# Latent attention of the odd layer: keys and values as products of the weight stream, heads as steps beside gates and output product

## What is computed

```python
cq, ckv, ik, iw, gate = _split_cols(z, [Q_LORA, KV_LORA, IDX_DIM, IDX_HEADS, DSA_WIDTH])
q = (_rmsnorm(cq, q_norm) @ w_qb).reshape(b, t, 16, 128)
q_lat = jnp.einsum('bthd,hdc->bthc', q, w_uk)
ckv = _rmsnorm(ckv, kv_norm)
# for each query the 64 tokens with the highest index score, among those not later than it
s = jnp.einsum('bqhc,bqkc->bqhk', q_lat, ckv[sel]) * 128 ** -0.5
p = softmax(s)
o_lat = jnp.einsum('bqhk,bqkc->bqhc', p, ckv[sel])
o = jnp.einsum('bthc,hcd->bthd', o_lat, w_uv).reshape(b, t, 2048)
return (o * jax.nn.silu(gate)) @ w_out
```

## Time and profile before

| | us |
|---|---|
| median of 3 runs | 2896.55 (2895.43 to 2902.48) |
| the profiled execution | 2893.83 |
| its span, first to last instruction | 2892.0 |
| mean granted clock of TensorE | 0.998 of 2.4 GHz |
| busy: PE, DVE, ACT, POOL | 2857.4, 1879.2, 1417.9, 393.4 |
| transfers | 192 GB/s over the span |

### The profile page before, as it was taken

The page is one execution under the profiler, slowest core; times in us unless marked ns, Lnnn a source line. Parts: engine busy times, 40 slices in busy tenths (PEclk is TensorE's granted clock), DMA queues, the critical chain, the costliest instruction groups (busy, mean ns, idle before and its releaser), DMA issues.

```text
span 2892.0 us, 45428 instructions
## 1 busy us (share of the span) xinstructions
PE 2857.4 (99%) x19064; PEld 2606.1 (90%) x19064; DVE 1879.2 (65%) x2575; ACT 1417.9 (49%) x1964; POOL 393.4 (14%) x444
## 2 busy tenths in 40 slices
PE   8999999999999999999999999999999999999998
PEld 8999988998899988989998899898889999988997
DVE  6998655766566655778666666588555555555555
ACT  5445645456455555444444445654545444444444
POOL 0000000000000000008873663043000000000000
PEclk9999999999999999999999999999999999999999
DMA  7555455552555545567776666585655555555553
GB/s 244 190 195 172 155 189 187 188 178 74 187 195 172 171 168 175 193 202 248 238 245 216 231 230 211 186 258 165 204 190 184 195 191 194 198 190 192 197 194 131
DMA packets 288043, 558.45 MB, mean 193 GB/s; under 512 B 27424, under 2 KB 35872, under 8 KB 287584
## 3 DMA queue, kind: packets, MB, share of 16 engines
q1 hardware_dynamic: 281376, 531.27, 55.7%
q0 software_dynamic: 5456, 21.73, 1.9%
q10 hardware_dynamic: 1008, 2.55, 0.3%
HBM read 530.34 MB, written 25.17 MB: 192 GB/s over the span
## 4 chain that ended last, share of the span: by engine, by line
PE 92%; DVE 4%; ACT 2%; issue 1%; POOL 0%; DMA 0%; ACTq 0%; DVEq 0%; POOLq 0%
PE G L506 86%; PE T L506 4%; DVE WL L1648 1%; ACT WH L1071 1%; DVE Y L1656 1%; PE T L585 1%; PE G L979 0%; ACT SC_e L1074 0%; DVE X L1648 0%; DVE ST L1729 0%; DVE SC_e L1656 0%; ACT L1068 0%; POOL ZZ L2428 0%; DMA X<-in_x 0%; PE T L964 0%
## 5 line engine op out<-in xcount | busy, mean ns | idle before, releaser
L1648 DVE TENSOR_TENSOR WL<-RAW,WH 128x1024 fp32r<-128x1024 f32 (+1 forms) x948 | 1183.8, 1258 | 754.7 <-ACT WH L1071 745.3
L1071 ACT ACTIVATE WH<-RAW 128x1024 fp32r<-128x1024 f32 (+1 forms) x948 | 993.8, 1055 | 1027.4 <-PE G L506 1025.5
L506 PE MATMUL G<-A1h,WH 128*128 128x256 f32 (+1 forms) x2583 | 717.9, 279 | 1.6 <-DVE WL L1648 1.6
L506 PE MATMUL G<-A1l,WH 128*128 128x256 f32 x2560 | 710.7, 278 | 0.0
L506 PE MATMUL G<-A1h,WL 128*128 128x256 f32 x2560 | 709.4, 277 | 0.0
L506 PEld LDWEIGHTS G<-A1h,WH 128*128 128x128 f32 x2583 | 485.7, 188 | 5.1 <-DVE WL L1648 2.9
L506 PEld LDWEIGHTS G<-A1l,WH 128*128 128x128 f32 x2560 | 482.3, 188 | 0.4
L506 PEld LDWEIGHTS G<-A1h,WL 128*128 128x128 f32 x2560 | 482.4, 188 | 0.0
L506 PE MATMUL G<-WH,Bh 128*128 128x512 f32 x1024 | 399.3, 390 | 0.6 <-DVE WL L1648 0.6
L506 PE MATMUL G<-WH,Bl 128*128 128x512 f32 x1024 | 398.5, 389 | 0.0
L506 PE MATMUL G<-WL,Bh 128*128 128x512 f32 x1024 | 398.5, 389 | 0.0
(11 more groups left out here) (325 smaller groups left out, 3564.6 us busy)
## 6 DMA issues: line engine op xcount, KB each, us to landing
RAW<-in_mlp_w SPq DMA_DIRECT2D x256, 1024.0 KB, 5.4
RAW<-in_even_w_in SPq DMA_DIRECT2D x52, 1024.0 KB, 5.0
RAW<-in_a_w_in SPq DMA_DIRECT2D x48, 1024.0 KB, 5.2
RAW<-in_b_w_glu SPq DMA_DIRECT2D x32, 1024.0 KB, 5.4
RAW<-in_odd_w_in SPq DMA_DIRECT2D x20, 1024.0 KB, 5.0
RAW<-in_even_w_out SPq DMA_DIRECT2D x16, 1024.0 KB, 5.1
RAW<-in_odd_w_out SPq DMA_DIRECT2D x16, 1024.0 KB, 5.1
RAW<-in_a_w_out SPq DMA_DIRECT2D x16, 1024.0 KB, 5.0
```

The costliest lines, as they stand in the source:

```text
L506: return e.matmul(out, lhsT, rhs, start=start, stop=stop, skip_group_check=True)
L1071: return e.activation(out, in_, ACT.Copy, scale=scale, bias=0.0)
L1648: return e.tensor_tensor(out, a, b, op)
```

## The change

Keys and values of four heads at a time become products `kk0` to `kk3` and `vv0` to `vv3` of the weight stream, one half each, with the latent in two parts (`CKTh`, `CKTl`). A chunk holds the key weights of four heads in its first half and their value weights in the second. For a key half PE transposes the weights from `RAW` to two of the banks `T` (`turn_keys`, steps in `gate1` and after it), and ACT and DVE split from there; a value half is split as any other. ACT evacuates both to `KTo` and `VO`, which now hold all heads. The order is `gate1`, `kk0`, `vv0`, ... `vv3`, `gate2`, `gate3`, `oo0`. The heads are steps beside the halves from `kk2` on, one slot of `HEADS_O` behind each: the scores of the heads in slots 0, 1, 3, 4, 6, 7, ... 15, 16, 18, 19, 20, 21, the shares one slot later, turn two and output three slots later. Slots 20 to 27 fall in `oo0`. The bank pairs are dealt in the other order up to `gate3`.

```diff
-    turn = itertools.cycle((0, 2))
+    turn = itertools.cycle((2, 0))
...
+    def latent_weights(g):
+        for tag, fm in ((f"kk{g}", True), (f"vv{g}", False)):
+            first_chunk[tag], STEPS[tag] = len(chunks), 1
+            bank = next(turn)
+            G_of[tag] = G[bank:bank + 2]
+            SHAPE[tag] = (2, 512, fm, [0])
+        second_half.add(f"vv{g}")
+        latent_chunk[len(chunks)] = g
+        chunks.append((None, (4, 512), True))
...
-    for i in range(1, 4):
+    weights("gate1", wo, 2048, 848 + 512, fm=True, steps=1)
+    for g in range(4):
+        latent_weights(g)
+    for i in range(2, 4):
         weights(f"gate{i}", wo, 2048, 848 + 512 * i, fm=True, steps=1)
-    next(turn)
...
-    HEADS_O = [{k: r - d for k, d in (("weights", 0), ("keys", 1), ("scores", 2), ("turn", 3), ("values", 3), ("pv", 4))
-                if 0 <= r - d < 16} for r in range(20)]
+
+    HEADS_O = [[] for _ in range(28)]
+    for _h, _n in enumerate((0, 1, 3, 4, 6, 7, 9, 10, 12, 13, 15, 16, 18, 19, 20, 21)):
+        for _d, _s in ((2, "turn"), (3, "pv"), (0, "scores"), (1, "shares")):
+            HEADS_O[_n + _d].append((_s, _h))
...
-        for i in range(1, 4):
-            if i == 3:
-                beside(first_rounds_o())
+        def heads_o():
+            for steps in HEADS_O:
+                for what, h in steps:
...
+                    fresh[0] = True
+                yield
+
+        def turn_keys():
+            for g in (None, 0, None, 1, None, None, None, 2, None, 3):
+                if g is not None:
+                    T, c = TB[2 * (g % 2):2 * (g % 2) + 2], first_chunk[f"kk{g}"]
+                    if g < 2:
+                        e.wait_ge(*o_d["ix", 13 + 2 * g])
+                    else:
+                        e.wait_ge(*w_lo[first_half(f"kk{g - 2}")])
+                    e.wait_ge(*w_in[c % NR][c])
+                    for j in range(2):
+                        for h in range(4):
+                            at = 256 * h + 128 * j
+                            m = e.transpose(T[j][:, 128 * h:128 * h + 128], RAW[:, c % NR, at:at + 128], IDENT)
+                    m.then_inc(*uk_t.up(g))
+                    fresh[0] = True
+                yield
+
...
+        beside(turn_keys())
+        gemm("gate1", A1h, A1l)
+        for g in range(4):
+            if g == 2:
+                finish()
+                beside(heads_o())
+            gemm(f"kk{g}", CKTh, CKTl, None if g else (lambda kt: e.wait_ge(*o_l["ckt"])))
+            gemm(f"vv{g}", CKTh, CKTl)
+        for i in range(2, 4):
             gemm(f"gate{i}", A1h, A1l)
-        finish()
-        for heads in HEADS_O[3:16]:
-            round_o(heads)
-        beside(last_rounds_o())
         for i in range(4):
-            if i == 1:
-                e.wait_ge(*k_c[15])
             gemm(f"oo{i}", A2ho, A2lo, None if i else (lambda kt: e.wait_ge(*o_l["o", kt])))
             beside(norm_block("a", i, f"oo{i}"))
         finish()
...
+            if n in key_half:
+                T = TB[2 * (key_half[n] % 2):2 * (key_half[n] % 2) + 2]
+                e.wait_ge(*uk_t[key_half[n]])
+                e.wait_ge(*w_read[n - RS])
+                copy(WH[:, n % RS, 0:512], T[0][:, :])
+                copy(WH[:, n % RS, 512:1024], T[1][:, :]).then_inc(*w_hi.up(n))
+                return
+            if h == 0 or c < NR or c in latent_chunk:
...
+        def latent(g):
+            gemm(f"kk{g}")
+            take_fm(f"kk{g}", KTo, 4 * g)
+            gemm(f"vv{g}")
+            for i in range(2):
+                e.wait_ge(*whole_bank(f"vv{g}", i))
+                copy(VO[:, 4 * g:4 * g + 4, i, :], G_of[f"vv{g}"][i][:, :].rearrange("p (h d) -> p h d", d=128)).then_inc(
+                    *ev_a.up((f"vv{g}", i)))
+
+        gemm("gate1")
+        silu_fm("gate1", GT, 4)
+        for g in range(4):
+            if g == 2:
+                beside(heads_o())
+            latent(g)
+        for i in range(2, 4):
             gemm(f"gate{i}")
...
-        finish()
-        for heads in HEADS_O[3:16]:
-            round_o(heads)
-        beside(last_rounds_o())
...
+            if n in key_half:
+                T = TB[2 * (key_half[n] % 2):2 * (key_half[n] % 2) + 2]
+                for j in range(2):
+                    d = tt(WL[:, n % RS, 512 * j:512 * j + 512], T[j][:, :], hi[:, 512 * j:512 * j + 512], ALU.subtract)
+                d.then_inc(*w_lo.up(n))
+                return
...
+        def heads_o():
+            for steps in HEADS_O:
+                for what, h in steps:
+                    st = 8 + 8 * (h % 2)
+                    if what == "scores":
+                        if h >= 2:
+                            e.wait_ge(*p_t["o", h - 2])
+                        maxima(TB[0], PP[h % 2], MM[:, :], st, ("o", h))
+                    elif what == "shares":
+                        shares(PP[h % 2], st, ("o", h))
+                    elif what == "pv":
+                        e.wait_ge(*pv_mm["o", h])
+                        if h % 4 == 0:
+                            e.wait_ge(*act2[f"gate{h // 4}", 1])
+                        tt(GT[:, h, :], TB[3][:, 0:256], GT[:, h, :], ALU.mult).then_inc(*o_d.up(("o", h)))
+                        e.wait_ge(*o_h["o", h])
+                        low(A2lo[:, h, :], GT[:, h, :], A2ho[:, h, :]).then_inc(*o_l.up(("o", h)))
...
-        for i in range(1, 4):
-            if i == 3:
+        gemm("gate1")
+        take_fm("gate1", GT, 4)
+        for g in range(4):
+            if g == 2:
                 finish()
-                beside(first_rounds_o())
+                beside(heads_o())
+            gemm(f"kk{g}")
+            gemm(f"vv{g}")
...
             take_fm(f"gate{i}", GT, 4 * i)
-        finish()
-        for heads in HEADS_O[3:16]:
-            round_o(heads)
         tt(GP, col("final", 0, 16), col("norm_mix", 0, 16), ALU.mult).then_inc(*d_step.up("gp"))
-        beside(last_rounds_o())
...
+            if c in latent_chunk:
+                g = latent_chunk[c]
+                e.dma_start(RAW[:, c % NR, 0:1024].rearrange("p (h c) -> p h c", c=256),
+                            t["odd_w_uk"][0, 4 * g:4 * g + 4].rearrange("h d c -> d h c")).then_inc(*w_in[c % NR].up(c, 16))
+                for k in range(2):
+                    at = 1024 + 512 * k
+                    e.dma_start(RAW[:, c % NR, at:at + 512].rearrange("p (h d) -> p h d", d=128),
+                                t["odd_w_uv"][0, 4 * g:4 * g + 4, 128 * k:128 * k + 128].rearrange("h p d -> p h d")).then_inc(
+                        *w_in[c % NR].up(c, 16))
+                return
```

More of the change, by code:

```diff
@@ L771, in pe @@
         finish()
[L773 to L828, removed]
@@ L1312, in prep_o @@
                     e.wait_ge(*t_mm["ckv"])
-                    copy(CKT[:, :, :], pairs(TB[2][:, :])).then_inc(*a_step.up("ckt"))
+                    copy(CKTh[:, :, :], pairs(TB[2][:, :])).then_inc(*o_h.up("ckt"))
                 elif what == "turn_ik":
@@ L1328, in act @@
             take_fm(f"qb{i}", QTo, 4 * i)
[L1330 to L1343, removed]
-                copy(KTo[h % 2], G[0][:, 0:256]).then_inc(*k_c.up(h))
-            if "turn" in heads:
-                h = heads["turn"]
-                e.wait_ge(*p_t["o", h])
-                if h >= 2:
-                    e.wait_ge(*pv_mm["o", h - 2])
-                copy(PT[h % 2], TB[1][:, 0:384]).then_inc(*p_c.up(("o", h)))
-            if "scores" in heads:
-                h = heads["scores"]
-                exps(PP[h % 2], 8 + 8 * (h % 2), ("o", h))
-            if "pv" in heads:
-                h = heads["pv"]
-                e.wait_ge(*o_d["o", h])
-                copy(A2ho[:, h, :], GT[:, h, :]).then_inc(*o_h.up(("o", h)))
-            if "values" in heads:
-                h = heads["values"]
-                e.wait_ge(*v_mm[h])
-                if h >= 2:
-                    e.wait_ge(*pv_mm["o", h - 2])
-                copy(VO[h % 2], TB[2][:, 0:256].rearrange("p (a b) -> p a b", b=128)).then_inc(*v_c.up(h))
@@ L1365, in first_rounds_o @@
-        def first_rounds_o():
-            for r in range(3):
-                yield
-                round_o(HEADS_O[r])
-                yield
-        def last_rounds_o():
-            for heads in HEADS_O[16:]:
-                round_o(heads)
-                yield
-        for i in range(1, 4):
-            if i == 3:
-                beside(first_rounds_o())
+        def heads_o():
+            for steps in HEADS_O:
+                for what, h in steps:
+                    if what == "turn":
+                        e.wait_ge(*p_t["o", h])
+                        if h >= 2:
+                            e.wait_ge(*pv_mm["o", h - 2])
+                        copy(PT[h % 2], TB[1][:, 0:384]).then_inc(*p_c.up(("o", h)))
+                    elif what == "scores":
+                        exps(PP[h % 2], 8 + 8 * (h % 2), ("o", h))
+                    elif what == "pv":
```

(6 more changed lines are left out.)

95 lines of the change are left out of this document (38 added, 57 removed).

## The result

| | before | after |
|---|---|---|
| median, us | 2897.14 (4 runs, 2895.43 to 2902.48) | 2920.94 (4 runs, 2912.98 to 2924.79) |
| the profiled execution | 2893.83 | 2912.98 |
| its span | 2892.0 | 2911.2 |
| start of `gate1`, start of `oo1` | 566.35, 714.01 | 564.63, 732.53 |
| between the two ("the stage") | 147.66 | 167.90 |

The change makes the kernel slower: the ratio is 1.0075, 95% interval 1.0050 to 1.0101. A second set of five runs gave 2919.17 beside 2897.09, 1.0080 (1.0067 to 1.0094). The prediction had 2918, with +21.6 us in the stage; the stage has +20.2.

The account below looks back on a forecast made before the run. Hand-overs between ACT and DVE were taken to bound the stage: PE's -5.6 us and 27 us of waiting gave +21.6, so 2896.55 + 21.6 = 2918 us, range 2907 to 2929.

Parts of the forecast that it names:

- Bound and direction: In the stage, hand-overs between ACT and DVE set the period and PE waits; slower by 21.6 us, chance of slower 0.88.
- PE's own sum: PE's work in the stage: weights, keys, values and a wait removed; products, transposes and interruptions added; -5.6 us.
- The start: From `gate1` to slot 4: `kk2` ends at 606.1, `vv3` waits 3 us, slot 4 starts on ACT at 626.7.
- The slots: Heads beside halves: three slots take 5.67, 6.42 and 1.90, together 13.99 us, where PE needs 11.7.
- The gates' evacuations: Evacuations of `gate2` and `gate3` on ACT between slots: 2.36 us each, as in the first layer.
- The clock: Every matmul in the stage taken at the rows' speed; a granted clock under 1.00 would break the sum.
- Slot 22 and the end: Slot 22 starts at 719.3, head 15's shares are done at 723.6, PE reaches `oo1` at 735.6, before 714.0.
- The time: Whole kernel: 2896.55 + 21.6 = 2918 us; the forecast itself, 2913 to 2923, had 0.68.
- Rival 1: In the stage, PE stays the bound and the change gains: -5.3 us, 2891; chance 0.10.
- Rival 2: In the stage, splits three halves ahead hide 8.2 us of the lag: +13.3, 2910; chance 0.12.
- Rival 3: In `gate1`, chunks land late and add up to 5 us of wait: 2920 to 2926; chance 0.10.

Follow-up runs that it names:

- e1: Changed kernel with ACT splitting the next half ahead of the exponentials in slots with scores; stage 143.60 us, median 2894.43, ratio to the kernel before 0.9988.
- e4: Changed kernel with DVE forming the low part of each head's output twice; stage 174.19 us, median 2923.36, ratio to the kernel before 1.0087.
- e5: e3 with DVE forming the low part of each head's output twice; stage 145.22 us, median 2895.21, ratio to the kernel before 0.9993.
- e6: Changed kernel with the heads in denser slots (scores in 0 to 7, 9 to 12, 17 to 20); stage 172.56 us, median 2922.55, ratio 1.0090.
- e8: e3 with the heads in the denser slots of e6; stage 142.73 us, median 2896.22, ratio to the kernel before 0.9985.
- e3: Changed kernel with both ACT's split and its latent evacuations ahead of the exponentials; stage 142.91 us, median 2895.37, ratio to the kernel before 0.9991.
- e2: Changed kernel with ACT's evacuations of `kk` and `vv` ahead of the exponentials, splits unmoved; stage 165.56 us, median 2917.18, ratio 1.0068.
- e9: Changed kernel with ACT's split ahead of the exponentials for heads 0 to 7 alone; stage 157.81 us, median 2907.60, ratio 1.0028.
- e7: Changed kernel with the heads in rounds alone between `gate3` and `oo0`, not beside halves; stage 176.67 us, median 2927.75, ratio 1.0106.

## Why the prediction was right, and where its terms were off

- *Bound and direction.* Right. ACT and DVE in turn set the period, PE waits for shares and for copies. e1 shows the mechanism by taking it away, e4 and e5 by adding to it, e6 and e8 by the place of the heads.
- *PE's own sum, -5.6.* Right: 142.9 where it gives 142.1 (e3). A `kk` half took 3.0 (601.98 to 604.95) for the assumed 2.9; three slots take 11.84 in e1 for 11.7.
- *The start.* PE ended `kk2` 40.3 us into the stage (predicted 39.8), `kk3` waited 0.39 (0.4), `vv3` 2.42 (3), slot 4 began on ACT at 60.5 (60.35).
- *The slots.* ACT's splits come 1.32, 6.06 and 6.24 apart (631.39, 632.71, 638.77, 645.01), where I had 1.90, 5.67 and 6.42. DVE is still at the shares of the short slot until 634.27, so what that slot doesn't take the next one does. Period 13.62 for 13.99. DVE's low part lasts 0.43 in the earlier trace rows, but the next instruction starts 0.34 behind it (636.30, 636.64), twice a period; the shares were 0.1 dear as well. Four periods: 1.5 us too much; the other slots, 0.7.
- *The gates' evacuations, 2.36 each.* Mis-sized for `gate2`. The rows on ACT:

```profile
658.63 1.04 ACT L1062 ACTIVATE WH<-RAW 128x1024 fp32r<-128x1024 f32 x1
...
660.07 1.28 ACT L1059 ACT_TABLE_LOAD   x1
662.22 1.23 ACT L1059 ACTIVATE GT<-GT 128x512 f32<-128x512 f32 x2 [0.87 <-DVE GT L1624]
663.36 1.04 ACT L1062 ACTIVATE WH<-RAW 128x1024 fp32r<-128x1024 f32 x1
...
702.63 1.28 ACT L1059 ACT_TABLE_LOAD   x1
703.92 1.15 ACT L1059 ACTIVATE GT<-GT 128x512 f32<-128x512 f32 x2
704.98 1.04 ACT L1062 ACTIVATE WH<-RAW 128x1024 fp32r<-128x1024 f32 x1
```

  For `gate3` ACT was free at 702.6 and split at 704.98, 2.4 as in the earlier trace rows. For `gate2` it waited 0.87 more: DVE's part of the evacuation stood behind the shares of a head (split 659.71, shares 660.85, its product with the rows' scale 661.50). 663.36 - 658.63 for a slot that else takes 1.32 is 3.4, 1.0 too little in the sum; 0.4 of it come back in the next slot, which takes 5.67 and not 6.06. The Trainium skill's 2.66 for a switch of tables (ScalarE: Activation LUTs, What ACT_TABLE_LOAD costs) is not seen: the load of `gate3` lasts 1.28, and the SiLU starts 1.29 after the load started.
- *The clock.* The prediction took every matmul at full clock and said that a lower one would break its sum. There were three falls, 5.1 us of clock, and the sum held: the two inside the periods cost nothing at the end (e2), since PE would have waited there anyway. For the first, behind `vv3`, ACT still began slot 4 at 60.5, where the sum without it has 60.35; no run takes it away alone. It is luck of this kernel that no fall came behind the last wait, where e2 lost 1.5 by one.
- *Slot 22 and the end.* 151.6 and 167.9 into the stage (predicted 153.0 and 169.3): -1.5 and -0.7 for the slots, +0.6 for `gate2` and +0.2 for the start make the difference.
- *The time.* 2918 is 3 us under the median, while the stage is 1.4 us under its sum. The two go opposite ways because executions also differ by several us outside the stage, which the sum doesn't cover; that 2918 fell so near is in part luck. The range's own terms give 2908 to 2928, not 2907 to 2929.
- *Start of the stage.* It lies 1.7 us earlier than before, which no step had; the last section has the row. It is not in the sum, which starts at `gate1`.
- *Rival 1* (PE stays the bound) had the wrong mechanism for this kernel, and 2891 for its time; with one instruction of ACT moved PE is the bound, at 2894. The rule that I set beside it (the Trainium skill, Perfetto Trace Analysis, Identifying the Most-Contended Engine: work on the engine with the highest occupancy, for TensorE judged by MFU and LDWEIGHTS busy) doesn't tell these kernels apart: PEld is 90% busy before, after and in e1, over 26 us of difference. The edit that pays takes PE's waits away, but it is made on ACT, 49% busy. *Rival 2* (three halves of cover): against it stand e9 and the period itself. *Rival 3* (late chunks): PE never waits for a DMA ahead of the key transposes.

Of the 5.6 us of PE's own gain 4.1 and 4.7 reach the end of the stage in e1 and e3. The ratios are 0.9988 and 0.9991: for e1 a gain just clear of noise, for e3 one whose interval ends at 1.0000. The change as it was made loses 22 to 24.

## What to carry to other kernels

Where two engines pass work to and fro in the order written, add up the hand-overs of one period, who waits for whom, and compare that with the bound engine's period; the busy shares don't show it. Put what another engine will want next (here a split that had its input and its buffer ready) ahead of what you would have to wait for anyway. A cost that such a chain takes in full may be mostly hidden once the order is right (6.3 us became 2.3 with e5, 4.6 became none with e8), so mend the order before work is cut or slots are moved.

## What the runs showed of the hardware

**The clock fell behind some waits of about 2 us, and a wait's length doesn't say which.** PE's waits of 0.4 to 0.7 in each period left the granted clock at 1.00; the three falls of after came with waits of 2.42, 2.02 and 1.89. A wait of 2.24 (719.82) had none, but in e2 the same wait of 2.24 had one, while its wait of 2.00 (673.78), the counterpart of the 2.02, had none. In e7 the heads' rounds keep PE 58% busy with a wait of 1.5 in each. Windows of it at the start of the rounds, among them, and at their end:

```profile
666.00:673.00 7.00, 5.79 (x22) 5.03 (x22) 4.71 (x15) 3.56 (x14) 0.00 (x0) 0.51 0.00 0
680.00:690.00 10.00, 5.83 (x33) 4.53 (x33) 7.08 (x24) 4.33 (x16) 0.00 (x0) 1.00 0.00 0
717.00:724.00 7.00, 6.21 (x20) 4.84 (x19) 3.32 (x8) 2.16 (x4) 0.00 (x0) 0.53 0.00 0
```

The clock stayed up through eleven waits of 1.5 in a row, and was at its lower level for nearly 7 us at either end, behind waits of 2.36 and 2.29. A fall cost nothing at the end of the stage where PE had another wait ahead of it (twice in after), and 1.5 us (e2) or 1.7 (e7) where it had not.

**The same products run at two paces with the clock at 1.00.** Windows of 85 us over the same products of the third layer, in the first execution of after and in the second:

```profile
2210.00:2295.00 85.00, 85.00 (x738) 84.47 (x737) 47.83 (x47) 40.28 (x46) 0.00 (x0) 1.00 0.60 198
```

```profile
2213.00:2298.00 85.00, 85.00 (x724) 85.00 (x723) 46.01 (x44) 38.68 (x43) 0.00 (x0) 1.00 0.57 192
```

The counts miss some records, but the starts agree: eleven matmuls in a row start from 2249.80 to 2250.93 in the one, 0.113 apart, and from 2253.75 to 2254.93 in the other, 0.118. From one split of ACT to another, the same two in both, the first takes 88.27 us (2207.93 to 2296.20) and the second 91.64 (2210.73 to 2302.37): 3.4 us between two executions of one kernel. Another 1.6 of their 6.2 us come near 335, where the clock falls in the second execution (0.79 from 332 to 340) and not in the first (1.00). Most of the earlier start of the stage, 1.3 of 1.7 us, arises from 340 to 378, and is a difference of pace too: windows of before and of the first execution of after over the same products:

```profile
348.00:366.00 18.00, 18.00 (x155) 18.00 (x154) 12.03 (x15) 9.48 (x11) 0.00 (x0) 1.00 0.37 133
```

```profile
348.00:366.00 18.00, 18.00 (x161) 18.00 (x160) 11.27 (x13) 9.89 (x12) 0.00 (x0) 1.00 0.46 159
```

Why a stretch has the one pace or the other stays open. The stage took 167.90 and 167.94 in the two executions of after, and is the better measure of this change than the median.
